# Attention of a hybrid diffusion step: VectorE divides pairs of heads, each between the masks of two pairs of a later half tile

## The reference

```python
def _attend(q, k, v, valid, sink):
    s = jnp.einsum('bqgrd,bkgd->bgrqk', q, k).astype(jnp.float32) * (HEAD_DIM ** -0.5)
    if valid is not None:
        s = jnp.where(valid[None, None, None], s, NEG_INF)
    ...
    p = jax.nn.softmax(jnp.concatenate([s, sk], axis=-1), axis=-1)[..., :-1]
    return jnp.einsum('bgrqk,bkgd->bqgrd', p.astype(v.dtype), v)
```

## Time and profile before

| | us |
|---|---|
| median of 3 runs | 5839.04 (5838.94 to 5841.78) |
| the profiled execution | 5846.38 |
| its span, first to last instruction | 5844.6 |
| attention stage, layer 1, first matmul to start of the last copy out | 355.94 to 450.65 |
| attention stage, layer 2, the same | 3223.41 to 3320.20 |

### The profile page before, as it was taken

The page is one execution under the profiler, slowest core; times in us unless marked ns, Lnnn a source line. Parts: engine busy times, 40 slices in busy tenths (PEclk is TensorE's granted clock), DMA queues, the critical chain, the costliest instruction groups (busy, mean ns, idle before and its releaser), DMA issues. The chain is left out here.

```text
span 5844.6 us, 118044 instructions
## 1 busy us (share of the span) xinstructions
PE 5424.8 (93%) x47828; PEld 5213.8 (89%) x47828; DVE 3252.5 (56%) x6038; ACT 2191.8 (38%) x2761; POOL 2133.7 (37%) x968
## 2 busy tenths in 40 slices
PE   7977888999999999999989688889999999999999
PEld 3856788999999999999977577889999999999998
DVE  5545648646654156666644564775556522666665
ACT  4433322555555422222233432235555563222221
POOL 0001222656656533343300012236555654433332
PEclk8989999999999999999999899999999999999999
DMA  6100112455555654545411001225555556455443
GB/s 247 58 25 11 62 55 85 143 170 172 178 168 171 210 193 161 169 164 171 142 63 52 17 5 61 87 92 164 168 172 167 180 164 228 166 173 172 162 168 108
DMA packets 303870, 777.73 MB, mean 133 GB/s; under 512 B 23596, under 2 KB 109100, under 8 KB 299368
## 3 DMA queue, kind: packets, MB, share of 16 engines
q1 hardware_dynamic: 303464, 771.94, 39.2%
HBM read 586.52 MB, written 185.34 MB: 132 GB/s over the span
## 5 line engine op out<-in xcount | busy, mean ns | idle before, releaser
L2169 POOL TENSOR_TENSOR ex_v_lo<-ex_v_raw,ex_v_hi 128x1024 fp32r<-128x1024 f32 x256 | 692.1, 2725 | 1071.1 <-ACT ex_v_hi L2075 1071.1
L344 PE MATMUL ex_ps<-tk_h_hi,tk_u_hi 128*128 128x320 f32 x4096 | 968.4, 318 | 43.6 <-POOL tk_u_lo L2157 35.1
L344 PE MATMUL ex_ps<-tk_h_hi,tk_u_lo 128*128 128x320 f32 x4096 | 940.9, 311 | 26.8 <-issue 26.8
L2157 POOL TENSOR_TENSOR tk_u_lo<-tk_u_raw,tk_u_hi 128x1024 fp32r<-128x1024 f32 x256 | 643.4, 2514 | 882.0 <-ACT tk_u_hi L2045 881.7
L344 PE MATMUL ex_ps<-ex_wa_hi,ex_v_hi 128*128 128x320 f32 x4096 | 935.2, 310 | 18.8 <-issue 18.8
L344 PE MATMUL ex_ps<-tk_h_lo,tk_u_hi 128*128 128x320 f32 x4096 | 938.8, 311 | 0.0
L344 PE MATMUL ex_ps<-ex_wa_lo,ex_v_hi 128*128 128x320 f32 x4096 | 934.6, 309 | 0.0
L344 PE MATMUL ex_ps<-ex_wa_hi,ex_v_lo 128*128 128x320 f32 x4096 | 934.5, 309 | 0.0
L2329 DVE TENSOR_TENSOR ex_y<-ex_y,ex_ps 128x640 f32<-128x640 f32 x496 | 405.9, 818 | 671.3 <-PE ex_ps L344 666.5
L344 PEld LDWEIGHTS ex_ps<-tk_h_hi,tk_u_hi 128*128 128x128 f32 x4096 | 682.7, 190 | 45.6 <-POOL tk_u_lo L2157 36.0
L344 PEld LDWEIGHTS ex_ps<-tk_h_hi,tk_u_lo 128*128 128x128 f32 x4096 | 690.8, 189 | 27.5 <-issue 27.5
(11 more groups left out here) (323 smaller groups left out, 7783.2 us busy)
## 6 DMA issues: line engine op xcount, KB each, us to landing
tk_u_raw<-in_expert_u SPq DMA_DIRECT2D x256, 512.0 KB, 4.4
ex_v_raw<-in_expert_v SPq DMA_DIRECT2D x256, 512.0 KB, 3.5
act_spill<-tk_act_e SPq DMA_DIRECT2D x256, 320.0 KB, 2.3
grid_scratch<-tk_grid SPq DMA_DIRECT2D x160, 512.0 KB, 5.7
ex_g<-grid_scratch SPq DMA_DIRECT2D x64, 1280.0 KB, 10.5
x<-in_w_mod_rows SPq DMA_DIRECT2D x192, 256.0 KB, 4.8
ex_a<-act_spill SPq DMA_DIRECT2D x32, 1280.0 KB, 6.3
x<-act_spill SPq DMA_DIRECT2D x32, 1280.0 KB, 6.3
```

Of the source, the lines that this page charges most:

```text
L344: ins = nc.tensor.matmul(out[:, q, 0:HALF], a, b[:, q * HALF:(q + 1) * HALF], start=(first and n == 0), stop=(last and n == 2))
L2157: nc.gpsimd.tensor_tensor(u_lo[:, at % 2], u_raw[:, at % 3], u_hi[:, at % 2].bitcast(F32), ALU.subtract).then_inc(e["u_split"], 1)
L2169: nc.gpsimd.tensor_tensor(v_lo[h][:, k], v_raw[:, k], v_hi[h][:, k].bitcast(F32), ALU.subtract).then_inc(e["v_split"], 1)
```

## The change

On VectorE, `front` is split into `masked_pair(part, q)`, which masks two heads, and `tops(part)`, the two small instructions behind all four. `back` becomes `divide(part, q)`: sum, inverse and two multiplications for one pair. It waits for the exponentials of its pair (3 of the part's 5 for the first pair, all 5 for the second). The masks now wait for the transposes of the old slot head by head. The loop's order becomes: masks of the first pair of part p + 2, division of the first pair of part p + 1, masks of the second pair of p + 2, `tops(p + 2)`, division of the second pair of p + 1. So a division is now issued one iteration ahead of the transposes that need it. The copy out of a tile stands one part earlier. The other engines' code is not touched.

```diff
-                def front(part):
+                def masked_pair(part, q):
                     sink = s.pvs("sink")[:, PART * (part % 2):PART * (part % 2) + PART]
-                    if part >= SLOTS:
-                        dve.wait_ge(pt_ready, 4 * (part - SLOTS) + 4)
-                    for h in range(PART):
+                    for h in (2 * q, 2 * q + 1):
+                        if part >= SLOTS:
+                            dve.wait_ge(pt_ready, 4 * (part - SLOTS) + h + 1)
                         dve.wait_ge(scores, 4 * part + h + 1)
                         v.tensor_tensor_reduce(...).then_inc(masked, 1)
+
+                def tops(part):
...
-                def back(part):
-                    dve.wait_ge(exped, 5 * part + 5)
-                    v.tensor_tensor(den[:, part], den[:, part], sink_e[:, part], ALU.add).then_inc(den_ready, 1)
-                    dve.wait_ge(den_ready, part + 1)
-                    v.reciprocal(den[:, part], den[:, part]).then_inc(inverse, 1)
-                    dve.wait_ge(inverse, part + 1)
-                    for h in range(PART):
+                def divide(part, q):
+                    pair = slice(2 * q, 2 * q + 2)
+                    dve.wait_ge(exped, 5 * part + 2 * q + 3)
+                    v.tensor_tensor(den[:, part, pair], den[:, part, pair], sink_e[:, part, pair], ALU.add).then_inc(den_ready, 1)
+                    dve.wait_ge(den_ready, 2 * part + q + 1)
+                    v.reciprocal(den[:, part, pair], den[:, part, pair]).then_inc(inverse, 1)
+                    dve.wait_ge(inverse, 2 * part + q + 1)
+                    for h in (2 * q, 2 * q + 1):
                         v.tensor_scalar(sm[:, part % SLOTS, h, :], sm[:, part % SLOTS, h, :], den[:, part, h:h + 1], None,
                                         ALU.mult).then_inc(probs, 1)
...
-                front(0)
-                front(1)
+                for part in range(2):
+                    for q in range(2):
+                        masked_pair(part, q)
+                    tops(part)
+                for q in range(2):
+                    divide(0, q)
                 for part in range(N):
-                    back(part)
-                    if part + 2 < N:
-                        front(part + 2)
-                    if part >= 3 and part % 2:
-                        take((part - 3) // 2)
+                    for q in range(2):
+                        if part + 2 < N:
+                            masked_pair(part + 2, q)
+                            if q:
+                                tops(part + 2)
+                        if part + 1 < N:
+                            divide(part + 1, q)
+                    if part >= 2 and part % 2 == 0:
+                        take(part // 2 - 1)
                 take(TILES - 1)
```

More of the change, by code:

```diff
@@ L880, in front @@
                                                sink[:, h:h + 1], ALU.add, ALU.max, top[:, part, h:h + 1]).then_inc(masked, 1)
+                def tops(part):
+                    sink = s.pvs("sink")[:, PART * (part % 2):PART * (part % 2) + PART]
                     dve.wait_ge(masked, 4 * part + 4)
```

## The result

| | before | after |
|---|---|---|
| median, us | 5840.41 (5838.94 to 5843.8, 4 runs) | 5807.01 (5796.05 to 5810.76, 4 runs) |
| ratio | | 0.9939 [0.9922, 0.9956] |
| profiled execution, us | 5846.38 | 5803.98 |
| its span, us | 5844.6 | 5802.2 |
| attention stage, layer 1 / 2, us | 96.27 / 98.35 | 76.25 / 76.10 |

The change makes the kernel faster by 0.6%. It fell by 20.02 and 22.25 us, together 42.3, and the two profiled executions differ by 42.4. That these two agree is luck: between the same two executions the input projections got 3.1 and 2.9 us shorter, the scan of layer 1 3.6 us longer and the retrieval of layer 1 3.1 us longer, and these cancel.

What follows compares the result with a forecast made beforehand. TensorE and VectorE waiting for each other through program order bound the attention. Parts 0 to 7 (-17.60, -20.71) and the ends (-2.56, -1.59) gave -42.5, -40.9 with one clock fall left in: from 5839.0 to 5798, 8 in 10 5791 to 5813.

Steps and rivals of the forecast that it cites:

- Step 1: VectorE's division issued ahead: done by paths of 4.72 and 3.20 us, both under 6.22 a part, so TensorE never waits.
- Step 2: Loop through ScalarE's sinks and copies, next to bind: 5.78 us a part, 0.44 under TensorE's 6.22.
- Step 3: VectorE's own work: 5.92 us a part with 0.40 for the added sum and inverse, hidden under 6.22.
- Step 4: Second semaphore waits on three of four masks: at most 0.11 us each, 0.33 a part, taken as 0.
- Step 5: Copy out one part earlier, into VectorE's slack: price 0; its former 0.60 us in every second part goes.
- Step 6: Falls of TensorE's clock in the attention, 1.56 us lost in one: should go once TensorE's idle times go.
- The sum: Attention stages: part 0 6.82 us, parts 1 to 7 43.54, the end 10.07; in all -42.5 for two layers.
- TensorE isn't the floor: Rival, chance 0.04: TensorE packs its queue to 4.80 us, VectorE's 5.92 becomes the period; 5794.
- VectorE becomes the bound: Rival, chance 0.15: VectorE, nearly full, can't absorb late scores; a part takes 7.2 us; 5812.
- The clock falls as often: Rival, chance 0.09: TensorE's clock falls as often as before and each costs in full; 5804.
- Slower: Rival, chance 0.04: pairs go one behind the other through three engines, 9.44 us a part, +16.5; 5856.
- No change: Rival, chance 0.04: loop over the sinks takes in the path from transposes to masks, 8.08 us a part; 5836.

Runs made afterwards that it cites:

- pairs_in_place: Against the kernel before: division split by pairs, each issued right ahead of the transposes that need it, not a part ahead; 5871.29 us, ratio 1.0038 to before.
- whole_ahead: Against the changed kernel: division's call moved one part ahead but kept as one block of four heads behind all four masks; 5852.15 us, ratio 1.0004 to before.
- slot_wait_once: The changed kernel with the wait for the old slot's transposes once in a part, not for each head; 5806.06 us, ratio 0.9924 to before.
- copy_out_late: The changed kernel with the copy out of a tile a part later, where it stood before; 5812.14 us, ratio 0.9921 to before.
- live_blocks: The changed kernel without computing key blocks that the mask hides for all queries of a tile, same results; 5780.03 us, ratio 0.9866 to before.
- tensor_less: The changed kernel without the value products of the cached keys, so part of the output is left out; 5767.03 us, ratio 0.9849 to before.
- vector_plus_two: The changed kernel with two multiplications of 128x512 added to VectorE behind `tops` in each of parts 2 to 9; 5809.62 us, ratio 0.9919 to before.
- again: The changed kernel run once more, unaltered; 5813.52 us, ratio 0.9932 to before.

## Why the prediction was right

The forecast was 5798 (5791 to 5813 for 8 in 10); 5807.01 was measured. That is inside this range but outside the forecast's own, 5792 to 5805, and by the number alone the rivals at 5804 and 5812 would have done as well. It is the traces that decide for the forecast's mechanism, which held in its steps, with the sizes of the stage:

- *Step 1, issued ahead.* TensorE waits for no multiplication in the middle parts. It waits for them 5.4 us in all, for the very first ones, where about 7 had been given. Of the two halves, dividing alone costs 0.4% (pairs_in_place). That being ahead needs the dividing was only argued: whole_ahead keeps the order of before, and a whole division that is really ahead, estimated at 7.3 for a part, was not run.
- *Step 2, what is late next.* The loop through sinks and copies, put at 5.78, did not bind: copies come 1.17 behind transposes where 1.5 was set as the mark. How near that loop is to binding was not tested.
- *Step 3, VectorE's part.* Put at 5.92, it is 5.76: the sum took 1.47 for each pair of masks, but that interval runs up to `tops`, and a pair that the division follows takes 1.34 (390.79 to 392.13). In parts: 1.34 + 1.46 + 2 x 1.19 + 0.28 + 0.30. The added sum and inverse, taken at 0.40, were right. By form, columns as count, busy us, mean ns, they are

```profile
L894 DVE RECIPROCAL at_den<-at_den 128x2 f32<-128x2 f32 x20 | 3.3, 166 | 0.7
...
L892 DVE TENSOR_TENSOR at_den<-at_den,at_sink_e 128x2 f32<-128x2 f32 x20 | 3.1, 156 | 2.5 <-ACT at_sm L931 2.5
```

  where 128x4 had 155 (L888) and 178 ns (L890). Half the columns save 12 ns of an inverse and nothing of a sum. The page "VectorE: DVE Perf Modes" of the Trainium skill, section on the TRN2 errata, gives VectorE's instructions a fixed cost, and by these two rows the trace agrees.
- *Step 4, added waits*: bounded at 0.11 for a mask and taken as 0. The 0.11 is real wherever VectorE waits for scores (slot_wait_once, whole_ahead); in the changed kernel the slack hides it, but for 0.1 us at the end of each layer. *Step 5, copy out*: 0 taken, 0 measured in copy_out_late.
- *Step 6, the clock*: 1.00 through parts 1 to 7 in both layers of the changed kernel. whole_ahead, which kept the pauses of 1.8 us, kept two such falls in either layer. One in its layer 1:

```profile
387.00:390.00 3.00, 3.00 (x22) 2.31 (x24) 1.22 (x4) 2.08 (x6) 0.00 (x0) 0.55 0.02 5
```

  pairs_in_place, with its pauses of 1.4 and 1.8, has them too (6.15 from 412.06 to the next transposes, where the pattern is 4.58), and in the ten profiles of kernels in the changed order whose transposes run without such pauses, parts 1 to 7 show none. That TensorE's pauses bring the falls is borne out by this, not proved. The low clock at the start of the stage, behind TensorE's long idle time there, is in all kernels: part 0 of the changed one has 0.67 and 0.81 in its halves, the one before had 0.70 and 0.79, and in live_blocks, where the first parts are short, the low clock reaches to 377.63.
- *The sum*: part 0 was put at 6.82 and measured at 6.82, parts 1 to 7 at 43.54 and 43.59, the end at 10.07 and 10.04 or 10.05. In all -42.5 was worked out before one fall was left in, and the stages gave -42.3. Leaving one fall in was caution that nothing asked for: there was none in parts 1 to 7. At the end two paths close together: part 9's transposes at 423.81 come 0.55 behind their multiplication (423.26), as the prediction has it, and the profile names the copy that frees their PSUM (422.73 and 1.08 long), which it didn't have.

Of the rivals, "TensorE isn't the floor" is refuted by tensor_less: taking 0.44 from TensorE took 0.44 from the part. In the changed kernel its weight loads are busy for 4.80 of 6.23 us, and yet it is TensorE that sets the part. The page "Perfetto Trace Analysis" of the Trainium skill, section Identifying the Most-Contended Engine, would have TensorE's headroom judged by the time of its weight loads, which is 77% here. For these short fp32 matmuls the trace disagrees with it: the matmuls' own busy time, 6.23 of 6.23, was the better sign. "VectorE becomes the bound" failed by about 0.5 us a part, which vector_plus_two used up. "The clock falls as often" failed by the granted clock of 1.00. "Slower" described a real loop, but of another order: it bites in pairs_in_place. "No change" came true for whole_ahead, but for another reason than the loop over the sinks: its order repeats as before.

What was off is the step from the stage to the whole. The forecast took the saving over from one execution to the median, since it "lies in stages that don't depend on what the rest took". The two stages don't, yet the rest scatters. Comparing stage by stage, the input projection of the one layer or the other takes 209.4 or 212.4 us (once 215.4), the stage between scan and retrieval 111.8, 113.3 or 115.0, with the same code and in either direction from run to run; the scan takes anything from 242.0 to 249.9. So medians of four or five runs move by ten us: -33.4 at first, -35.7 in the run again, with intervals of 0.14 to 0.17% (8 to 10 us) on either side that take in the -42.3 (a ratio of 0.9928). Whether the missing 7 to 9 us are this scatter alone can't be told from these runs; up to 5 of them may lie in the retrieval stages (see **again** above).

## What to carry to other kernels

When two engines wait for each other in turn, look at what stands in program order between a result and the wait that needs it: here a division whose data was ready waited behind masks that were waiting for scores. Interleave in the unit in which the other engine delivers, and issue each piece one such unit ahead of its last moment; divided but not ahead it lost here, and ahead but whole was not run. Compare stage by stage before comparing totals, for steps of 3 us in untouched stages hide a part of an effect of this size, and an edit elsewhere in TensorE's stream moved the total by as much as the whole change.

## What the runs showed of the hardware

- Instructions that do nothing useful made the kernel faster: 80 tiny matmuls far ahead of the expert loops took the idle "issue" time there from 55.6 to 28.4 us, and the retrieval stage from 2187.2 to 2167.6 us in layer 1 and from 2164.4 to 2143.7 in layer 2, 40 us in all between two profiles, about as much as the whole change; the medians on one chip, against copy_out_late, differ by 38. 13.6 us a layer of that are the idle time; the remaining 6 are matmuls that are shorter by 1 ns in the mean, 2048 in each of three groups (two go from 311 to 310 ns, one from 318 to 317). Eight kernels, before and after among them, have 54.1 to 57.4, four have 28.0 to 32.1, and live_blocks has 47.7. The profile doesn't name what TensorE waits for there, and neither do these runs; a supply of instructions that depends on where the code lies would fit and was not tested by itself. live_blocks and a shift together were not run.
- Two multiplications of 128x512 from one SBUF buffer to another hold VectorE for 0.67 us (397.10 to 397.77), where two in place, with a scale for each row, take 0.80 (389.39 to 390.19). Which of these differences does it was not tested.
- A second semaphore wait ahead of a mask of VectorE, on a count that had long been reached, costs 0.11 us where the engine stands waiting: 2.30 from transposes to masks with two waits (changed kernel, whole_ahead), 2.19 with one (before, slot_wait_once). Where VectorE has slack it doesn't lengthen the stage's parts.
